# Forward substitution in two 64-row halves in place of the last level of a block inversion, in the RWKV scan of a two-layer decoder

## The reference, cut to what matters

```
def step(S, inp):
    r_t, w_t, k_t, v_t, kk_t, a_t = inp
    sa = jnp.einsum('bhij,bhj->bhi', S, -kk_t)
    S = (S * w_t[:, :, None, :]
         + sa[..., None] * (kk_t * a_t)[:, :, None, :]
         + v_t[..., None] * k_t[:, :, None, :])
    y = jnp.einsum('bhij,bhj->bhi', S, r_t)
    return S, y
_, ys = lax.scan(step, S0, (tmajor(rh), tmajor(wh), tmajor(kh), tmajor(vh), tmajor(kk), tmajor(ah)))
```

## Time and profile before

| | us |
|---|---|
| median of 3 runs | 1505.27 |
| lowest and highest | 1505.21, 1505.7 |
| the profiled execution | 1507.26 |
| its span in the trace | 1505.4 |
| PE busy in the span | 1474.2 |
| DVE busy | 1242.6 |
| ACT busy | 1009.8 |

### The profile page before, as it was taken

How to read it: one execution, slowest core, us unless ns; L and a number is a source line. 1 busy time by engine, 2 the same in 40 slices (tenths; PEclk the granted TensorE clock), 3 DMA queues, 4 the chain that set the end, 5 groups by cost and what they waited for, 6 DMA issues and landing times.

```text
span 1505.4 us, 22041 instructions
## 1 busy us (share of the span) xinstructions
PE 1474.2 (98%) x8088; PEld 1226.9 (82%) x8088; DVE 1242.6 (83%) x1375; ACT 1009.8 (67%) x1157; POOL 22.2 (1%) x19
## 2 busy tenths in 40 slices
PE   8999999999899999999999999999999999999997
PEld 5888888799798588888888888888888888888885
DVE  3756666787885289999999999999999999999997
ACT  2544444663523178888888888888888878888885
POOL 0000000000000020000000000000000000000200
PEclk9999999999999999999999999999999999999998
DMA  9889553036405499999999999999999999999990
GB/s 361 326 271 301 175 168 112 1 117 217 141 2 178 174 322 372 395 392 395 396 392 396 394 368 388 390 365 383 394 366 373 393 386 362 395 380 362 349 369 28
DMA packets 206696, 453.57 MB, mean 301 GB/s; under 512 B 8881, under 2 KB 46257, under 8 KB 206386
## 3 DMA queue, kind: packets, MB, share of 16 engines
q1 hardware_dynamic: 203154, 446.12, 80.6%
q0 software_dynamic: 1280, 4.20, 1.1%
q10 hardware_dynamic: 2208, 2.50, 0.5%
HBM read 437.58 MB, written 23.60 MB: 306 GB/s over the span
## 4 chain that ended last, share of the span: by engine, by line
PE 92%; DVE 5%; ACT 2%; DMA 1%; issue 0%; DVEq 0%; ACTq 0%
PE psum L1591 20%; PE psum L1593 20%; PE psum L1592 20%; PE psum L2401 5%; PE psum L2404 3%; PE psum L902 2%; PE psum L2325 2%; PE psum L2365 2%; PE psum L2366 2%; PE psum L2367 2%; PE psum L600 2%; PE psum L1609 2%; PE psum L2318 1%; PE psum L696 1%; DVE time_mix_parts L1150 1%; PE psum L722 1%
## 5 line engine op out<-in xcount | busy, mean ns | idle before, releaser
L1799 DVE TENSOR_TENSOR w_lo<-ring,w_hi 128x1024 fp32r<-128x1024 f32 x672 | 811.0, 1224 | 63.5 <-ACT w_hi L1693 15.8
L1693 ACT ACTIVATE w_hi<-ring 128x1024 fp32r<-128x1024 f32 x672 | 711.3, 1062 | 172.5 <-PE psum L1593 172.4
L1591 PE MATMUL psum<-w_hi,xg_split 128*128 128x512 f32 x896 | 353.5, 395 | 0.3 <-DVE xg_split L1890 0.3
L1593 PE MATMUL psum<-w_lo,xg_split 128*128 128x512 f32 x896 | 349.4, 390 | 0.0
L1592 PE MATMUL psum<-w_hi,xg_split 128*128 128x512 f32 x896 | 348.8, 389 | 0.0
L1593 PEld LDWEIGHTS psum<-w_lo,xg_split 128*128 128x128 f32 x896 | 168.1, 188 | 35.8
L1591 PEld LDWEIGHTS psum<-w_hi,xg_split 128*128 128x128 f32 x896 | 168.3, 188 | 34.1 <-DVE xg_split L1890 0.6
L1592 PEld LDWEIGHTS psum<-w_hi,xg_split 128*128 128x128 f32 x896 | 168.4, 188 | 33.6
L1591 PE MATMUL psum<-w_hi,ht_split 128*128 128x512 f32 x448 | 176.0, 393 | 0.0
L1593 PE MATMUL psum<-w_lo,ht_split 128*128 128x512 f32 x448 | 174.6, 390 | 0.0
L1592 PE MATMUL psum<-w_hi,ht_split 128*128 128x512 f32 x448 | 174.4, 389 | 0.0
(11 more groups left out here) (370 smaller groups left out, 1488.7 us busy)
## 6 DMA issues: line engine op xcount, KB each, us to landing
ring<-o_moe_wg_dram SPq DMA_DIRECT2D x56, 2048.0 KB, 10.8
ring<-o_moe_wu_dram SPq DMA_DIRECT2D x56, 2048.0 KB, 11.3
ring<-o_moe_wd_dram SPq DMA_DIRECT2D x56, 2048.0 KB, 11.3
ring<-e_ffn_wg_dram SPq DMA_DIRECT2D x11, 1024.0 KB, 5.5
ring<-e_ffn_wu_dram SPq DMA_DIRECT2D x11, 1024.0 KB, 8.7
ring<-e_ffn_wd_dram SPq DMA_DIRECT2D x11, 1024.0 KB, 11.1
expert_rows<-work SPq DMA_DIRECT2D x1, 8192.0 KB, 27.9
ring<-e_w_in_dram SPq DMA_DIRECT2D x2, 2048.0 KB, 18.1
```

The source lines that it names most:

```text
L1591: nc.tensor.matmul(dst, x_hi, hi, start=first, stop=False)
L1593: return nc.tensor.matmul(dst, x_hi, lo, start=False, stop=last_)
L1693: nc.scalar.activation(w_hi[:, (4 * i + n) % 4, :], piece(i, n), ACT.Copy).then_inc(m_hi, 1)
L1799: V.tensor_tensor(w_lo[:, r, :], piece(i, n), w_hi[:, r, :].bitcast(F32), ALU.subtract).then_inc(m_lo, 1)
```

## The change

1. The last level (`turned(c, 2)`, `top_Y`, `top_X` and their copies) is gone, and X is no longer formed as a whole. Only its two 64x64 diagonal halves are kept, in tiles of 64 columns. U is found in two halves: R of the upper 64 rows, U of those, then R of the lower 64 rows with the product of A's lower left block and the upper U accumulated in PSUM, then U of those.
2. The levels work on tiles of 64 columns. `turned` is now two 64x64 products with 32 columns of the identity per head, in place of one 128x128 transpose. ACT copies per pair instead of per four heads, DVE's `spread`, `level_Y` and `level_X` handle half the columns or half the instructions.
3. `right_side` and `solved` are called per half (`rows` is `top` or `low`). U is copied by ACT instead of DVE, into the place of the old `Y6`.
4. The new state is made per head as 64x64 products into half a bank, and DVE copies the two diagonal blocks, scaled, into `ST`, which ACT has zeroed before. Chunk 1 no longer waits for the state before its third `turned`, but before `level_X(1, 0)`.
5. GpSimd's memset of `Y6` is gone; ACT zeroes three tiles of 128x1024 instead of two of 128x2048; the constants are 128 columns narrower; on DVE `masked(0, g)` stands one place earlier; SP's second expert load waits for all eight `solved` steps instead of four.

```diff
-            def top_Y(c):
...
-            def top_X(c):
...
             def turned(c, v):
-                for gg in range(4):
+                for pair in range(2):
...
-                    for l in range(4):
-                        last = nc.tensor.transpose(psum[:, TURN_BANK[gg], l * P:(l + 1) * P], XT[c][:, gg, l, :], ident)
+                    for gg, l, k, o, at in heads_of(pair):
+                        for hs in tops:
+                            even = ident[:, hs].rearrange("p (b h t) -> p b h t", h=2, t=B0 << v)[hs, :, 0, :]
+                            last = nc.tensor.matmul(psum[hs, pair, at // 2:at // 2 + 32], XT[c][hs, gg, l, :], even,
+                                                    start=True, stop=True)
...
+            top, low = slice(0, HD), slice(HD, P)
+
+            def solved(c, pair, rows):
+                if rows == top:
+                    pe.wait_ge(l_xd, lev(c, 1, pair))
+                    pe.wait_ge(t_rc, 4 * c + pair + 1)
+                else:
+                    pe.wait_ge(t_rc, 4 * c + 2 + pair + 1)
+                for gg, l, k, o, at in heads_of(pair):
+                    last = nc.tensor.matmul(psum[rows, 4 + pair, at:at + HD], XT[c][rows, gg, l, :],
+                                            Rs[rows, gg, HD * l:HD * l + HD], start=True, stop=True)
+                last.then_inc(t_u, 1)
+
+            def right_side(c, pair, rows):
+                pe.wait_ge(a_pm, 4 * c + 2 * pair + 2)
+                if rows == low:
+                    pe.wait_ge(t_uc, 4 * c + pair + 1)
+                upto = slice(0, rows.stop)
+                for gg, l, k, o, at in heads_of(pair):
+                    dst = psum[rows, pair, at:at + HD]
+                    vv = v_row[upto, c * D + k * P + o:c * D + k * P + o + HD]
+                    last = nc.tensor.matmul(dst, A_all[c][upto, gg, l, 2, rows], vv, start=True, stop=(c == 0 and rows == top))
+                    if c == 1:
+                        last = nc.tensor.matmul(dst, AR[:, k, c, 0, rows], ST[:, k, o:o + HD], start=False, stop=(rows == top))
+                    if rows == low:
+                        last = nc.tensor.matmul(dst, A_all[c][top, gg, l, 0, low], Us[top, gg, HD * l:HD * l + HD],
+                                                start=False, stop=True)
+                last.then_inc(t_r, 1)
...
-                            nc.tensor.matmul(dst, b_row[:, tile], Us[:, k // 2, P * (k % 2):P * (k % 2) + P], start=True, stop=False)
-                            last = nc.tensor.matmul(dst, k_row[:, tile], v_row[:, tile], start=False, stop=True)
+                        for gg, l, k, o, at in heads_of(pair):
+                            dst = psum[o:o + HD, 4 + pair, (k % 4) * HD:(k % 4 + 1) * HD]
+                            part = slice(k * P + o, k * P + o + HD)
+                            nc.tensor.matmul(dst, b_row[:, part], Us[:, gg, HD * l:HD * l + HD], start=True, stop=False)
+                            last = nc.tensor.matmul(dst, k_row[:, part], v_row[:, part], start=False, stop=True)
...
-            turned(0, 2)
-            right_side(0, 0)
-            pe.wait_ge(y_zero, 3)
-            top_Y(0)
+            right_side(0, 1, top)
+            solved(0, 0, top)
+            solved(0, 1, top)
             block_rows(1, 4)
-            right_side(0, 1)
-            top_X(0)
-            pe.wait_ge(rec_done, 2)
-            solved(0)
+            for pair in range(2):
+                right_side(0, pair, low)
+            for pair in range(2):
+                solved(0, pair, low)
             outputs(0)
...
-            turned(1, 2)
-            right_side(1, 0)
-            top_Y(1)
-            right_side(1, 1)
-            top_X(1)
-            solved(1)
+            pe.wait_ge(y_zero, 3)
+            for rows in (top, low):
+                for pair in range(2):
+                    right_side(1, pair, rows)
+                for pair in range(2):
+                    solved(1, pair, rows)
             outputs(1)
```

More of the change, by code:

```diff
@@ L743, in rwkv_pe @@
             products(15)
[L745 to L752, removed]
-                        last = nc.tensor.matmul(dst, AR[:, k, c, 0, :], ST[:, k, o:o + HD], start=False, stop=True)
-                last.then_inc(t_r, 1)
             pe.wait_ge(a_ma, 16)
@@ L817, in solved @@
-            def solved(c):
-                for pair in range(2):
-                    pe.wait_ge(t_rc, 2 * c + pair + 1)
-                    pe.wait_ge(l_x6, 2 * c + pair + 1)
-                    for gg, l, k, o, at in heads_of(pair):
-                        last = nc.tensor.matmul(psum[:, (6, 0)[c] + pair, at:at + HD], XT[c][:, gg, l, :],
-                                                Rs[:, gg, HD * l:HD * l + HD], start=True, stop=True)
-                    last.then_inc(t_u, 1)
+            top, low = slice(0, HD), slice(HD, P)
@@ L1093, in rwkv_act @@
             for v in range(2):
-                nc.scalar.activation(r3(ru(6 + v), U // P), ident.unsqueeze(1).to_broadcast([P, U // P, P]), ACT.Copy,
+                nc.scalar.activation(r3(ru(6 + v, 1024), 8), ident.unsqueeze(1).to_broadcast([P, 8, P]), ACT.Copy,
                                      scale=0.0).then_inc(y_zero, 1)
+            nc.scalar.activation(ST, ident.unsqueeze(1).to_broadcast([P, KT, P]), ACT.Copy, scale=0.0).then_inc(y_zero, 1)
             turned(0, 0)
             turned(0, 1)
-            turned(0, 2)
-            right_side(0, 0)
-            top_Y(0)
-            right_side(0, 1)
-            top_X(0)
+            for half in range(2):
+                for pair in range(2):
+                    right_side(0, pair, half)
+                for pair in range(2):
+                    solved(0, pair, half)
             outputs(0)
@@ L1112, in rwkv_act @@
             last.then_inc(gw_done, 1)
-            turned(1, 2)
-            right_side(1, 0)
-            top_Y(1)
-            right_side(1, 1)
-            top_X(1)
+            for half in range(2):
+                for pair in range(2):
+                    right_side(1, pair, half)
+                for pair in range(2):
+                    solved(1, pair, half)
             outputs(1)
@@ L1314, in level_X @@
                 dve.wait_ge(l_xu, lev(c, v, pair))
[L1315 to L1325 removed]
+                odd = halves(XT[c], pair, w, 1)
+                V.tensor_tensor(odd, odd, psum[:, 4 + pair, 0:256].rearrange("p (m b t) -> p m b t", m=8, t=w),
+                                ALU.add).then_inc(l_xd, 1)
             def gn_centre(c, bank):
@@ L1378, in rwkv_dve @@
                 dve.wait_ge(t_s, pair + 1)
-                for k in range(4 * pair, 4 * pair + 4):
-                    last = V.scalar_tensor_tensor(out=ST[:, k, :], in0=psum[:, 4 + pair, (k % 4) * P:(k % 4 + 1) * P],
-                                                  scalar=fac[:, k:k + 1], in1=C("heads"), op0=ALU.mult, op1=ALU.mult)
+                ks = slice(4 * pair, 4 * pair + 4)
+                for o in (0, HD):
+                    hs = slice(o, o + HD)
+                    last = V.tensor_tensor(ST[hs, ks, hs], r3(psum[hs, 4 + pair, 0:4 * HD], 4),
+                                           fac[hs, ks].unsqueeze(2).to_broadcast([HD, 4, HD]), ALU.mult)
                 last.then_inc(t_sc, 1)
```

157 lines of the change are left out of this document (55 added, 102 removed).

## The result

| | us |
|---|---|
| the changed kernel, median of 4 runs | 1533.12 (1532.06 to 1534.24) |
| the kernel before, median of 4 runs beside it | 1505.41 (1505.21 to 1505.7) |
| ratio, with its 95% interval | 1.0184 (1.0166 to 1.0202) |
| span of the profiled execution | 1530.2, before 1505.4 |
| mean granted clock in it | 0.977, before 0.996 |

The change makes the kernel 1.8% slower. The prediction was 1507.2 us with a range of 1499.5 to 1512, so it was wrong, and by far more than any term of its sum.

What follows compares the result with a forecast made beforehand. PE, with 92% of the chain, was taken to bound the kernel. The terms -1.05 - 1.1 + 0.6 - 0.5 - 0.35 - 0.7 + 5.0 gave +1.9 us on the median of 1505.27: 1507.2 us, range 1499.5 to 1512.

Steps and rivals of the forecast that it cites:

- The price of a turn: In right_side, a product between products of another form (64 or 128 rows) costs 0.259 us instead of 0.117, 0.142 more.
- The lower bound of 0.232: Lowest price in us of a 64*64 product standing between products of another form, from the second start of L783.
- free rows: Rival, chance 0.12: a change of rows alone costs nothing, so 96 products save 13.6 us and the kernel takes 1493.6 us.
- half price: Rival, chance 0.08: changes of form in right_side cost half, 6.8 us less, so the kernel takes 1500.4 us.
- The sum at full clock: All seven parts together, +1.9 us on the median of 1505.27 and rounded to 1507.2 us; likeliest case, chance 0.70.
- zeroing: ACT's first zeroing writes, halved in size, let PE start chunk 0's levels at 413.41 instead of 414.46: -1.05 us.
- -1.1 + 0.6 - 4.5 - 0.5: Chunk 0, first level product to last state product: levels -1.1, solving +0.6, state -0.5; -4.5 takes out the turns.
- -0.35 - 0.7 + 5.0 - 9.1: Chunk 1, levels to outputs: start -0.35, levels -0.7, solving +5.0; -9.1 takes out the turns.
- The state: Chunk 0's new state: 16 products at 0.117 us, 1.87 per pair, before 1.98, and fewer changes of form: -0.5 us.
- the other end: Cheaper state in the likeliest case: alternating column halves load in parallel, 0.93 us per pair, 1.9 us less in all.
- third rival: Chance 0.10: the clock falls in the solving stretches' alternating products, 1.6 us a fall; three falls give 1512 us.
- Costed at nothing: ACT's copies of R and U in solving, hidden behind the other pair's products; uncovered, up to 0.6 us per step change.

Runs made afterwards that it cites:

- e2: The changed kernel, but in chunk 1 the upper half's product of A and v takes all 128 rows: 1515.38 us, 1.0059 of the kernel before.
- e5: The changed kernel with right_side's products kind by kind and the loads of wo and the router's weights issued later: 1495.36 us, 0.9928 of the kernel before.
- e1: The changed kernel, but right_side does its products kind by kind for a pair's 8 heads instead of head by head: 1506.99 us, 1.0000 of the kernel before.
- e4: The changed kernel, but the loads of wo and the router's weights start after chunk 1's last level_Y: 1526.84 us, 1.0132 of the kernel before.
- e7: e5 with chunk 0's lower right side again head by head, 64 and 128 rows in turn: 1503.99 us, 0.9988 of the kernel before.
- e10: e5 with only the second group of heads in chunk 0's lower right side going head by head: 1499.03 us, 0.9947 of the kernel before.
- e9: e5 with chunk 0's lower right side going two heads at a time: 1495.48 us, 0.9936 of the kernel before.

## Why the prediction was wrong, point by point

- **The price of a turn** (0.259 us a product, 0.142 over a like run): right, 0.26 in the changed kernel at 432.6 us, 0.63 us for a head in e2. The lower bound of 0.232 and the rivals of free rows and of half price are out.
- **The sum at full clock** (1507.2 us): no run shows the changed kernel at full clock. Worked out from e5, 1495.36 + 84 x 0.142 = 1507.3 us. Where the terms can be read in e5, they hold, too: zeroing -1.0 (predicted -1.05). From A to B the prediction without its turns is -1.1 + 0.6 - 4.5 - 0.5 = -5.5 us, and in e5 it measures -6.7; from B to C it is -0.35 - 0.7 + 5.0 - 9.1 = -5.1, and it measures -3.8. The first differs by the state, below; the second by the six changes that the order by kinds still has, 0.85 us, and 0.4 us that I can't place.
- **The state** (-0.5 for both groups): mis-sized. The likeliest price was 1.87 us per group, the other end 0.93, and the trace shows the other end: 0.94, so -2.1 us (rows below).
- **The clock** (third rival, 0.10, 1512 us): this is the step that failed, in three ways. The chance: it was held at 0.10 because `right_side` and `solved` of before keep 1.00. But those products have 128 weight columns (L822: 0.23 us each); none of them was like the new ones, and the prediction itself called the new ones sparse. All six stretches in strict turn that began at full clock lost it. Its example of a fall lies in a block of 128x128 transposes, where short falls come and go in other kernels too, so it was no measure of a long one. The length: it took one fall for some 3 us at half clock, as in the earlier trace rows, and measured are 17 and 48 us. The stretches with turns stay as thin at half clock (0.40 us a product), but e1 stays at half for 27.7 us without them, so why the clock comes back so late is not settled. The bound: 1.6 us a fall, three falls, 4.8 us, set the range's upper end; the clock cost 26.3 us in place of at most 4.8 (65 us at half, 0.4 us each).
- **The pause beside the loads** wasn't a rival at all: 1.5 us, and in chunk 1 it stands right before the second fall, which comes later without it (e4). The kernel before has the same loads in its levels, 361 GB/s from 452 to 462 us, and no such pause. Why, stays open: the new kernel's instructions come at another pace and its code lies elsewhere.
- **"Costed at nothing"**: ACT's copies of R and U are covered, as forecast; in e5 PE waits 0.2 us in the whole of A to C, and besides 0.7 us before `gn_mean`, as in the kernel before.

The chain of the kernel before, where one group's products for the state take from the first row to the second, 1.98 us, and the same in e5, 0.94 us:

```profile
447.18 0.42 PE psum L842 x2
...
449.16 0.38 PE psum L835 x4
```

```profile
442.28 0.12 PE psum L824 x2
...
443.22 0.22 PE psum L817 x4
```

The Trainium skill ("TensorEngine Tiling (Array Packing)", Key Properties) says that different tiles load weights and multiply in parallel. Here the products on alternating column halves do, 16 in 0.94 us. The prediction weighed that against a row (L836) in which 128 moving columns may set the pace, and went with the row; the row says nothing of 64.

Of the clock, the Trainium skill ("TensorE: Matmul & The Clock Gate", HAM oscillation — how this bites in real kernels) tells of falls that come from idle gaps of PE while it waits for data, with a cost of half the time at the low clock. In this case the fall in chunk 0 came with PE busy for 42.64 of 42.64 us, and the cost was some 0.4 of the time at half clock, not 0.5: a turning product goes from 0.26 to 0.40 us, one in a run of its like from 0.117 to 0.21 (e2, behind and before 481.7 us).

What stays open: in e1 the clock falls at about 455 us, between the pause of 0.41 us and that of 1.14 us. Whether the first pause or something else in the collision with the loads starts it was not separated; that it goes with the loads is shown by e5. How soon a stretch in turn loses the clock is not settled either: 1.4 us behind its first turn in the changed kernel, 1.8 in e7, 2.7 in e4 and 2.9 in e2, all with the same work in chunk 0, 4.1 us in e10, as the turns end, and 5.6 us in chunk 1 of e4.

## What to carry to other kernels

Put products of one form next to each other: accumulate kind by kind over a bank, not head by head. The same products cost 11.9 us less at full clock here, and 26 us more were lost to the clock that fell with the sparse order and the loads beside it. Two by two was already enough to keep the clock in chunk 0 here (e9), if the order can't be free. And read PE's pace from starts and counts, not from its busy share. Where products stand in strict turn as here (0.26 us apart, 64 weight and 64 moving columns), price a falling clock over the whole stretch and what follows it, at 0.4 us per microsecond, and not as a small risk of 1.6 us.

## What the runs showed of the hardware

- A change between products of 64 and 128 rows costs the same drain as other changes of form: 0.14 us each (1.68 us for 12 in e9, 0.63 us for a head with two of them in e2), and the other stretches of the table above fit it.
- The granted clock can fall while PE counts as busy without a break (e7: 42.73 of 42.73 us at a mean of 0.80), and it can stay at half for 27.7 us with products in runs of their like (e1).
- Products of 64 moving columns that alternate between the two column halves take 0.059 us each (16 in 0.94 us), where like ones in one column half take 0.117.
- PE can stand still for 0.4 to 1.8 us for no semaphore, shown as "issue" in the chain, in or right behind a stretch in which the 16 DMA engines carry 390 GB/s (e1, the changed kernel, e2); it doesn't when the loads start later (e4, e5). That it waits for its code is an inference.
